# Gathering and scaling the first expert's 32 slots ahead of the other 96, with the number of rounds read behind that

## The chip, the cores and the metric

The kernel runs on one core of one Trainium2 chip. The metric is the device time of one execution in microseconds (us); lower is better.

## What is computed

Two layers of a decoder trunk on 256 tokens of width 1024, all in float32. Each layer is a mixer of three attentions and then a mixture of experts (64 experts of width 256, two experts for each token), each followed by a LayerNorm:

```python
def reference(x, ...):
    for l in range(DEPTH):                       # DEPTH = 2
        mix = hybrid_mixer(x, w_in[l], ..., w_out[l])
        x = layer_norm(ALPHA * x + mix, ln1_g[l], ln1_b[l])
        ffn = moe_ffn(x, router_w, router_b, moe_w1[l], moe_w3[l], moe_w2[l])
        x = layer_norm(ALPHA * x + ffn, ln2_g[l], ln2_b[l])
    return x

def moe_ffn(x, router_w, router_b, w1, w3, w2):
    e_idx, gates = route(x, router_w, router_b)  # top-1 group of 8 experts, top-2 experts in it
    # for each expert e, over the tokens that chose it:
    #   h = silu(xb @ w1[e]) * (xb @ w3[e]);  y += gate * (h @ w2[e])
```

The change touches only the start of the expert stage.

## The kernel before

**Batches.** The 64 experts are worked through in batches of NB = 4, with BLK = 32 token slots for each expert, so P = 128 slots a batch: slots 0 to 31 are the first expert's, 32 to 63 the second's, and so on. 16 batches hold all experts; if an expert has more than 32 tokens, all batches are gone through again (a round). The number of batches is therefore known only once the tokens are counted. VectorE works it out (lines 1679 to 1682) and writes it into `iters`; every engine then reads it into a register with `start_batches` (lines 361 to 366), which waits for `routed` and loads the register (a TENSOR_LOAD in the trace). The loops over batches run up to that register.

**What a batch does on TensorE.** It gathers the batch's tokens: for each of DC = 8 chunks of 128 features, a matmul with the stream x as the weights and the one-hot matrix `chosen` (tokens by slots) as the moving operand, over NT = 2 tiles of 128 tokens. VectorE and ScalarE scale the result by the first LayerNorm's columns into `xg`. Then, for each expert, gate and up matmuls (32 slots as weights, w1 and w3 moving, four column groups of the array side by side), a fold over these groups, silu, a turn of the hidden rows, the down matmuls with w2, and `add_all` (line 1197), which adds the rows to the output in PSUM. The gather of the next batch is done inside each batch. Each float32 matmul is two instructions in the trace.

**The first batch** is written out by hand (`first_batch`, line 1202). Its gather is `gather_first` (line 1024): token tile 0 early, while the router still works on tile 1, and tile 1 when the choice is known. Its chunks lie in four PSUM banks (`first_bank`). Chunks 0, 1, 4 and 5 are scaled by VectorE and 2, 3, 6 and 7 by ScalarE, all 128 slots at once (`scale_first`). `first_up_gate` (line 1106) multiplies the first expert's 32 slots, first with w1 (gate, line 1119) and then with w3 (up, line 1124), in bank 2. `up_gate` (line 1092) does experts 1 to 3 (line 1102).

**Weights.** SyncE issues all weight transfers in one hand-written order. Two sets of buffers (even and odd batches) hold the weights of a batch, 12.6 MB. Batches 0 and 1 are loaded during the attention stage. The refills wait on TensorE:

```python
                def load_first(j, back, e, parity, last=False, by_matrix=False):
                    for k in range(NB):
                        if by_matrix and k == 0:
                            after(sp, l, gate_first, 1)
                            load_w13(e, k, parity, matrices=(0,))
                        done = 2 * (k // 2) + 2 if last else k + 1
                        sp.wait_ge(part_psum.sem, (b0 + j) * NB + (part_psum.start + done - back))
```

So the first matrix of batch 2 is loaded as soon as the first expert's gate matmuls are done (`gate_first`), its second when its up matmuls are done (`part_psum`), the next expert's when that expert's are done, w2 after the down matmuls. Batch 3's w1 and w3 (line 509) wait for batch 1's second expert.

## Time and profile before

| | |
|---|---|
| median of 3 runs | 1150.59 us (1150.25 to 1151.67) |
| profiled execution, its own time | 1149.66 us |
| its span | 1147.9 us |
| TensorE busy (matmul) | 1046.3 us, 91% of the span |
| TensorE busy (weight load) | 534.3 us, 47% |
| VectorE, ScalarE busy | 403.6 us, 260.3 us |
| DMA | 441.05 MB, 384 GB/s in the mean |

The span is that of the instructions; the execution's own time is 1.8 us longer. The page cuts the span into 40 slices of 28.7 us: slices 6 to 19 and 27 to 39 are the two expert stages. PE stands for TensorE, PEld for its weight loads, DVE for VectorE, ACT for ScalarE, SP for SyncE; an SPq row is an issue of DMAs by SyncE. Matmuls overlap, so the spacing of a row of them is its length over their count and not the duration of one.

### The profile page before, as it was taken

Reading aid. Unit: us, or ns where it says so; the run is one execution under the profiler, and the core shown is the slowest. Engines: PE = TensorE matmul, PEld = TensorE weight load, DVE = VectorE, ACT = ScalarE, POOL = GpSimd, SP = SyncE. Lnnn points to the kernel's source line nnn. Section 1 sums busy time; section 2 is a strip of 40 time slices with the busy share of each in tenths; the row PEclk is TensorE's granted clock in tenths of the full one; section 3 lists DMA queues with packets and bytes.
Section 4 is the critical chain, followed back from the end, with each engine's and each line's share of the span. In section 5 each row is a group of like instructions: output and inputs, shape, how many; then the busy total and the mean of one; then the engine's idle time right before and its main releaser. Section 6 shows DMA issues by size and latency. Waiting matters only on the chain.

```text
span 1147.9 us, 26691 instructions
## 1 busy us (share of the span) xinstructions
PE 1046.3 (91%) x11382; PEld 534.3 (47%) x11382; DVE 403.6 (35%) x1189; ACT 260.3 (23%) x683; POOL 18.7 (2%) x36
## 2 busy tenths in 40 slices
PE   9999999989889988888899999989889989988888
PEld 5665753434444443333466657434344444433333
DVE  4865532222222221222268656322222222222213
ACT  1245321111121111111131544121221111111111
POOL 0010000000000000000000100000000000000000
PEclk9999999999999999999999999999999999999999
DMA  9967699999999999999996677999999999999997
GB/s 307 330 249 293 256 400 406 428 426 425 426 428 429 429 429 429 429 429 420 387 319 227 268 297 278 403 426 425 426 426 429 428 428 429 428 429 428 429 421 268
DMA packets 72861, 441.05 MB, mean 384 GB/s; under 512 B 16480, under 2 KB 36064, under 8 KB 43616
## 3 DMA queue, kind: packets, MB, share of 16 engines
q1 hardware_dynamic: 72512, 439.52, 93.6%
q8 instruction: 46, 0.75, 0.3%
q0 software_dynamic: 144, 0.58, 0.1%
q14 instruction: 15, 0.12, 0.0%
q10 hardware_dynamic: 144, 0.07, 0.0%
HBM read 439.10 MB, written 1.05 MB: 383 GB/s over the span
## 4 chain that ended last, share of the span: by engine, by line
PE 73%; SPq 9%; DMA 9%; DVE 6%; issue 2%; ACT 1%; POOL 0%; DVEq 0%
PE bank L1087 13%; PE bank L1172 12%; PE bank L1184 8%; PE bank L693 8%; DMA w_odd<-in_moe_w 8%; PE bank L1069 7%; SPq L401 5%; PE bank L819 4%; PE bank L1102 3%; SPq L540 3%; PE bank L1137 2%; PE bank L1178 2%; DVE moe L1745 1%; PE bank L1056 1%; PE bank L963 1%
## 5 line engine op out<-in xcount | busy, mean ns | idle before, releaser
L1808 ACT ACTIVATE moe<-bank 128x512 f32<-128x512 f32 (+2 forms) x164 | 84.2, 523 | 555.8 <-PE bank L1087 275.5
L1709 DVE COPY moe<-bank 128x512 f32<-128x512 f32 x64 | 44.3, 692 | 315.6 <-PE bank L1087 256.9
L1184 PE MATMUL bank<-moe 128*128 128x512 f32 (+1 forms) x264 | 119.3, 593 | 23.6 <-DVE moe L1745 22.5
L1172 PE MATMUL bank<-w_even,moe 64*32 64x512 f32 x896 | 99.0, 590 | 10.1 <-DVE moe L1729 10.1
L1087 PE MATMUL bank<-w_odd,moe 64*32 64x512 f32 x1536 | 92.8, 629 | 11.2 <-issue 6.1
L1069 PE MATMUL bank<-moe,x 128*64 128x64 f32 x3072 | 98.3, 224 | 2.6 <-issue 2.6
L1069 PEld LDWEIGHTS bank<-moe,x 128*64 128x64 f32 x3072 | 94.8, 138 | 6.8 <-issue 6.8
L1745 DVE COPY moe<-bank 128x512 f32<-128x512 f32 x32 | 22.1, 692 | 198.7 <-PE bank L1172 178.0
L1184 PEld LDWEIGHTS bank<-moe 128*128 128x128 f32 x264 | 47.3, 190 | 96.0 <-DVE moe L1745 48.9
L1172 PE MATMUL bank<-w_odd,moe 64*32 64x512 f32 x768 | 84.8, 590 | 7.5 <-DVE moe L1729 7.5
L1087 PE MATMUL bank<-w_even,moe 64*32 64x512 f32 x1536 | 86.1, 591 | 5.9 <-issue 5.9
L693 PE MATMUL bank<-w_even,w_odd 128*128 128x384 f32 x240 | 81.3, 489 | 0.0
L1965 ACT ACTIVATE moe<-bank,small 128x64 f32<-128x64 f32 x192 | 59.3, 414 | 90.3 <-PE bank L1069 90.3
L1087 PEld LDWEIGHTS bank<-w_odd,moe 64*32 64x32 f32 x1536 | 30.2, 112 | 71.7 <-issue 71.7
L1172 PEld LDWEIGHTS bank<-w_even,moe 64*32 64x32 f32 x896 | 32.8, 107 | 65.5 <-issue 65.5
L1646 DVE TENSOR_SCALAR moe<-bank,small 128x64 f32<-128x64 f32 x192 | 50.6, 337 | 22.8 <-PE bank L1069 22.8
L693 PEld LDWEIGHTS bank<-w_even,w_odd 128*128 128x128 f32 x240 | 44.6, 190 | 29.1 <-issue 2.0
L1137 PE MATMUL bank<-moe,constants 128*32 128x512 f32 (+1 forms) x272 | 34.5, 576 | 25.3 <-DVE moe L1709 20.9
L1087 PEld LDWEIGHTS bank<-w_even,moe 64*32 64x32 f32 x1536 | 28.5, 107 | 61.7 <-issue 61.7
L1172 PEld LDWEIGHTS bank<-w_odd,moe 64*32 64x32 f32 x768 | 28.1, 107 | 54.9 <-issue 54.9
L1808 ACT ACTIVATE w_odd<-bank 128x256 f32<-128x256 f32 (+3 forms) x60 | 27.8, 468 | 83.2 <-PE bank L651 27.4
L819 PE MATMUL bank<-w_odd 128*128 128x512 f32 x96 | 44.8, 602 | 0.0
(203 smaller groups left out, 1013.5 us busy)
## 6 DMA issues: line engine op xcount, KB each, us to landing
w_even<-in_moe_w SPq DMA_DIRECT2D x76, 2048.0 KB, 36.4
w_odd<-in_moe_w SPq DMA_DIRECT2D x72, 2048.0 KB, 34.3
w_odd<-in_moe_w SPq DMA_DIRECT2D x44, 1024.0 KB, 10.2
w_even<-in_moe_w SPq DMA_DIRECT2D x40, 1024.0 KB, 9.6
w_even<-in_w_in SPq DMA_DIRECT2D x24, 768.0 KB, 11.0
w_odd<-in_w_out SPq DMA_DIRECT2D x4, 2048.0 KB, 13.6
w_odd<-in_moe_w SPq DMA_DIRECT2D x8, 512.0 KB, 11.1
w_even<-in_w_in SPq DMA_DIRECT2D x4, 416.0 KB, 6.8
```

What stands on the lines that cost most here:

```text
L401: sp.dma_start(w13_slots[parity][k][:, m, :, :].rearrange("p c f -> p (c f)"), (w1, w3)[m][l * NE + e * NB + k]).then_inc(sig.sem, 16)
L693: last = mm(to[:, 0:GW], rows[:, c, :], weights[:, c, :], start=fresh and c == 0, stop=c == DC // 2 - 1, skip_group_check=True)
L819: last = mm(mix_bank[t][h][:, :], oT[:, c, t * P:(t + 1) * P], w_out_half[h][:, c, :], start=c == 0, stop=c == DC - 1, skip_group_check=True)
L1069: last = mm(bank[2 + h][64 * z:64 * z + 64, 64 * c:64 * c + 64], xc_pair[:, t, h, c, :], chosen_pair[:, t, z], start=t == 0, stop=t == 1)
L1087: last = mm(bank[2 * q + z][BLK * i:BLK * (i + 1), :], xg_pair[rows, c, BLK * q:BLK * (q + 1)], w[rows, :, c, :], start=c < 4, stop=c >= 2 ...
L1137: last = mm(to[BLK * k:BLK * (k + 1), 0:cols.stop - cols.start], const("fold"), partial[:, k, cols], start=True, stop=True)
L1172: last = mm(bank[h][BLK * k:BLK * (k + 1), :], hT_pair[rows, c, BLK * q:BLK * (q + 1)], w2_pairs[parity][q][rows, c, 512 * h:512 * h + 512 ...
L1184: return mm(Y[t][h][:, lo - 512 * h:hi - 512 * h], scatter[:, t * P:(t + 1) * P], y_rows[:, lo:hi], start=False, stop=True, skip_group_che ...
L1646: last = ts(xg_pair[:, c, :], bank[2][:, 64 * c:64 * c + 64], pair_cols[:, 0, c:c + 1], pair_cols[:, 1, c:c + 1], ALU.mult, ALU.add)
L1709: nc.vector.tensor_copy(partial[:, k, :], source[:, :]).then_inc(part_dve.sem, 1)
L1808: return fn(dst, src, ACT.Copy)
L1965: last = fn(xg_pair[:, DC + c, :], bank[3][:, 64 * c:64 * c + 64], ACT.Identity, scale=pair_cols[:, 0, DC + c:DC + c + 1], bias=pair_cols[ ...
```

## The change

The first batch's gather of token tile 1 is split by slots. The first expert's 32 slots of all 8 chunks are gathered first, scaled (VectorE chunks 0 to 3, 6 and 7, ScalarE 4 and 5) and multiplied with the gate matrix. Between the gate and the up matmuls stands the gather of the other 96 slots. VectorE works out the number of rounds behind the first scales; a signal `counted` tells TensorE that bank 0 has been read. The remaining scales (VectorE chunks 0 to 3, ScalarE 4 to 7) must be done before the second expert. The register with the number of batches is read by SyncE behind the issues for batches 2 and 3, by TensorE behind the first batch, and by VectorE and ScalarE behind their scales. Chunks 2 and 3 move from bank 3 to the other half of bank 2, and the first expert's products from bank 2 to bank 3.

```diff
--- before.py
+++ after.py
@@ -265,7 +265,7 @@
         turn_bank = [bank[i] for i in (4, 5, 4, 5, 7, 7, 7, 7)]
         score_bank, pT_bank, o_bank = [bank[i] for i in (2, 3, 6, 7)], bank[4:6], bank[6]
         mix_bank = [bank[0:2], bank[2:4]]
-        first_bank = [bank[2], bank[3], bank[1][:, 2 * P:], bank[0][:, 2 * P:]]
+        first_bank = [bank[2], bank[2][:, 2 * P:], bank[1][:, 2 * P:], bank[0][:, 2 * P:]]
         Y = [[bank[4 + 2 * t + n] for n in range(2)] for t in range(NT)]
 
         class Signal:
@@ -321,8 +321,9 @@
         chosen_ok, xg_dve, xg_act = Signal("chosen_ok"), Signal("xg_dve"), Signal("xg_act")
 
         gate_first = Signal("first_gate_matrix_used", 1)
-        first_mid, first_late = Signal("first_batch_mid", 1), Signal("first_batch_late", 1)
-        first_begin_sb, first_mid_sb = Signal("first_batch_begin_sb", 1), Signal("first_batch_mid_sb", 1)
+        counted, first_late = Signal("tokens_counted", 1), Signal("first_batch_late", 1)
+        first_slots, first_slots_dve, first_slots_act = (
+            Signal("first_slots_psum", 3), Signal("first_slots_dve", 3), Signal("first_slots_act", 1))
         gathered = Signal("gathered_first_half"), Signal("gathered_second_half")
         part_psum, part_dve, part_act = Signal("part_psum", start=2 * NB), Signal("part_dve"), Signal("part_act")
         gu_psum, eg_ok, hn_ok = Signal("gu_psum"), Signal("eg_ok"), Signal("hn_ok")
@@ -489,7 +490,7 @@
                 load_w2(1, 1, 1)
                 after(sp, l, z_psum, 2)
                 load_w2(1, 0, 1)
-                m, b0 = start_batches(sp, base, l)
+                b0 = batches_before(sp, base)
 
                 def load_first(j, back, e, parity, last=False, by_matrix=False):
                     for k in range(NB):
@@ -525,6 +526,7 @@
                 load_w2_pairs(2, 0)
                 load_batch(3, 2 * NB, 3, 1)
                 load_w2_pairs(3, 1)
+                m, b0 = start_batches(sp, base, l)
                 with sp.Fori(4, m, 2) as j_even:
                     for parity in range(2):
                         j = j_even + parity
@@ -1021,19 +1023,22 @@
                 route(1, (4, 5), 7)
                 route(1, (6, 7), 8)
 
-                def gather_first(t):
+                def gather_first(t, lo, hi):
                     for c in range(DC):
-                        if c == 6:
-                            after(pe, l, *((routed, 1) if t else (z_lin, 2)))
-                        last = mm(first_bank[c // 2][:, c % 2 * P:(c % 2 + 1) * P], xc[:, t, c, :], chosen[:, t, :],
-                                  start=t == 0 and c in (0, 2), stop=t == 1, skip_group_check=True)
-                        if t == 1 and c % 2:
-                            last.then_inc((gathered[0], first_mid, first_late, gathered[1])[c // 2].sem, 1)
+                        if c == 6 and lo == 0:
+                            after(pe, l, *((counted, 1) if t else (z_lin, 2)))
+                        last = mm(first_bank[c // 2][:, c % 2 * P + lo:c % 2 * P + hi], xc[:, t, c, :],
+                                  chosen[:, t, lo:hi], start=t == 0 and c == 0, stop=t == 1, skip_group_check=True)
+                        if t == 1 and c in (3, 5, 7):
+                            if lo == 0:
+                                last.then_inc(first_slots.sem, 1)
+                            else:
+                                last.then_inc((gathered[0], first_late, gathered[1])[c // 2 - 1].sem, 1)
 
 
                 after(pe, l, n_ready, 1)
                 after(pe, l, chosen_first, 1)
-                gather_first(0)
+                gather_first(0, 0, P)
                 turn_rows(0)
                 keep_warm(7, bank[7])
                 after(pe, l, picked, 2)
@@ -1046,7 +1051,7 @@
                 keep_warm(2, bank[7])
                 after(pe, l, n_ready, 2)
                 pe.wait_ge(chosen_ok.sem, batches_before(pe, base) + 1)
-                gather_first(1)
+                gather_first(1, 0, BLK)
 
                 def gather(b):
 
@@ -1107,21 +1112,18 @@
                     pe.wait_ge(w13_in[0][0].sem, b0 * 8 + (32 + 32 * l))
                     w = w13_slots[0][0]
                     for c in range(DC):
-                        if c == 0:
-                            after(pe, l, first_begin_sb, 1)
-                        elif c == 2:
-                            after(pe, l, first_mid_sb, 1)
-                        elif c == 4:
-                            pe.wait_ge(xg_dve.sem, b0 + 1)
-                        elif c == 6:
-                            pe.wait_ge(xg_act.sem, b0 + 1)
+                        if c == 4:
+                            after(pe, l, first_slots_act, 1)
+                        elif c % 2 == 0:
+                            after(pe, l, first_slots_dve, c // 2 + 1 if c < 4 else 3)
                         q = c % 4
-                        last = mm(bank[2][BLK * q:BLK * (q + 1), 0:FE], xg[:, c, 0:BLK], w[:, 0, c, :],
+                        last = mm(bank[3][BLK * q:BLK * (q + 1), 0:FE], xg[:, c, 0:BLK], w[:, 0, c, :],
                                   start=c < 4, stop=c >= 4, skip_group_check=True)
                     last.then_inc(gate_first.sem, 1)
+                    gather_first(1, BLK, P)
                     for c in range(DC):
                         q = c % 4
-                        last = mm(bank[2][BLK * q:BLK * (q + 1), FE:2 * FE], xg[:, c, 0:BLK], w[:, 1, c, :],
+                        last = mm(bank[3][BLK * q:BLK * (q + 1), FE:2 * FE], xg[:, c, 0:BLK], w[:, 1, c, :],
                                   start=False, stop=c >= 4, skip_group_check=True)
                     last.then_inc(part_psum.sem, 1)
 
@@ -1201,6 +1203,8 @@
 
                 def first_batch():
                     first_up_gate()
+                    pe.wait_ge(xg_dve.sem, b0 + 1)
+                    pe.wait_ge(xg_act.sem, b0 + 1)
                     up_gate(0, 0, 1, 32 + 32 * l)
                     after(pe, l, seed_act, 1)
                     seed_rows(0)
@@ -1291,8 +1295,9 @@
                         after(pe, l, third_summed, t + 1)
                         add_rows(t, *fourth).then_inc(y_added.sem, 1)
 
+                b0 = batches_before(pe, base)
+                first_batch()
                 m, b0 = start_batches(pe, base, l)
-                first_batch()
                 batch(0, 1, 32 + 32 * l, pairs=False, next_pairs=False)
                 batch(2, 0, 48 + 32 * l)
                 batch(2, 1)
@@ -1676,22 +1681,25 @@
                 v.wait_ge(chosen_ok.sem, b0 + 1)
 
                 after(v, l, rank_psum, 3)
-                link(nc.vector.tensor_reduce(red[:, 0:1], bank[0][:, 2 * NE:3 * NE], X, ALU.max))
+                signal(nc.vector.tensor_reduce(red[:, 0:1], bank[0][:, 2 * NE:3 * NE], X, ALU.max), counted, 1)
+                after(v, l, cols_in, 160)
+
+                def scale_first(c, lo, hi):
+                    return ts(xg[:, c, lo:hi], first_bank[c // 2][:, c % 2 * P + lo:c % 2 * P + hi], g_cols[:, 0, c:c + 1],
+                              g_cols[:, 1, c:c + 1], ALU.mult, ALU.add)
+
+                for i, c in enumerate((0, 2, 6)):
+                    after(v, l, first_slots, 3 if c == 6 else 1)
+                    scale_first(c, 0, BLK)
+                    scale_first(c + 1, 0, BLK).then_inc(first_slots_dve.sem, 1)
                 link(ts(v1[:, 0, 0:MAX_ROUNDS - 1], const("thresholds"), red[:, 0:1], None, ALU.is_lt))
                 link(nc.vector.tensor_reduce(red[:, 1:2], v1[:, 0, 0:MAX_ROUNDS - 1], X, ALU.add))
                 signal(ts(iters[:, :], red[:, 1:2], float(BATCHES), float(BATCHES - 2), ALU.mult, ALU.add), routed, 1)
                 weigh_scores(1)
-                after(v, l, cols_in, 160)
-                def scale_first(c):
-                    return ts(xg[:, c, :], first_bank[c // 2][:, c % 2 * P:(c % 2 + 1) * P], g_cols[:, 0, c:c + 1],
-                              g_cols[:, 1, c:c + 1], ALU.mult, ALU.add)
-
                 v.wait_ge(gathered[0].sem, b0 + 1)
-                scale_first(0)
-                scale_first(1).then_inc(first_begin_sb.sem, 1)
-                after(v, l, first_late, 1)
-                scale_first(4)
-                scale_first(5).then_inc(xg_dve.sem, 1)
+                for c in range(4):
+                    last = scale_first(c, BLK, P)
+                last.then_inc(xg_dve.sem, 1)
                 m, b0 = start_batches(v, base, l)
 
                 def batch(j, last_of_all, e_next, first=False, pairs=False, w13_pairs=False, next_pairs=False):
@@ -1705,7 +1713,7 @@
                         choose_next()
                     for k in (0, 2):
                         v.wait_ge(part_psum.sem, b * NB + (part_psum.start + k + 1))
-                        source = bank[k if w13_pairs else 2 if first and k == 0 else 0]
+                        source = bank[k if w13_pairs else 3 if first and k == 0 else 0]
                         nc.vector.tensor_copy(partial[:, k, :], source[:, :]).then_inc(part_dve.sem, 1)
                         if first and k == 0:
                             weights(1)
@@ -1956,7 +1964,7 @@
                 route(1)
                 after(act, l, cols_in, 160)
                 seeds(0, range(DC))
-                m, b0 = start_batches(act, base, l)
+                b0 = batches_before(act, base)
 
                 def copy_gathered(g, pairs=False):
                     act.wait_ge(gathered[1].sem, g + 1)
@@ -1971,16 +1979,20 @@
                                   scale=g_cols[:, 0, c:c + 1], bias=g_cols[:, 1, c:c + 1])
                     last.then_inc(xg_act.sem, 1)
 
-                def scale_first(c):
-                    return fn(xg[:, c, :], first_bank[c // 2][:, c % 2 * P:(c % 2 + 1) * P], ACT.Identity,
+                def scale_first(c, lo, hi):
+                    return fn(xg[:, c, lo:hi], first_bank[c // 2][:, c % 2 * P + lo:c % 2 * P + hi], ACT.Identity,
                               scale=g_cols[:, 0, c:c + 1], bias=g_cols[:, 1, c:c + 1])
 
-                after(act, l, first_mid, 1)
-                scale_first(2)
-                scale_first(3).then_inc(first_mid_sb.sem, 1)
+                after(act, l, first_slots, 2)
+                scale_first(4, 0, BLK)
+                scale_first(5, 0, BLK).then_inc(first_slots_act.sem, 1)
+                after(act, l, first_late, 1)
+                scale_first(4, BLK, P)
+                scale_first(5, BLK, P)
                 act.wait_ge(gathered[1].sem, b0 + 1)
-                scale_first(6)
-                scale_first(7).then_inc(xg_act.sem, 1)
+                scale_first(6, BLK, P)
+                scale_first(7, BLK, P).then_inc(xg_act.sem, 1)
+                m, b0 = start_batches(act, base, l)
 
                 def copy_partial(b, k, source=bank[1]):
                     act.wait_ge(part_psum.sem, b * NB + (part_psum.start + k + 1))
```

## Rows read from the trace of the kernel before

**Rows 1.** The page: the span, and GB/s of the DMA in 40 slices.

```profile
span 1147.9 us, 26691 instructions
...
GB/s 307 330 249 293 256 400 406 428 426 425 426 428 429 429 429 429 429 429 420 387 319 227 268 297 278 403 426 425 426 426 429 428 428 429 428 429 428 429 421 268
```

**Rows 2.** The chain that ended last: start us, us, what.

```profile
125.97 1.73 PE bank L974 x16
...
149.56 1.72 PE bank L1102 x14
...
172.47 3.44 PE bank L1184 x8
175.90 7.05 PE bank L1102 x64
...
545.28 19.30 DMA w_odd<-in_moe_w
...
713.28 1.79 PE bank L1028 x16
715.07 1.49 PE bank L1119 x14
...
1112.89 19.04 DMA w_odd<-in_moe_w
```

**Rows 3.** Timeline of SyncE's issues: start us, us, what.

```profile
148.74 8.97 SPq L401 DMA_DIRECT2D w_even<-in_moe_w  x8
...
179.61 4.23 SPq L509 DMA_DIRECT2D w_odd<-in_moe_w  x4
193.24 0.80 SPq L411 DMA_DIRECT2D w_odd<-in_moe_w  x2
201.57 4.15 SPq L509 DMA_DIRECT2D w_even<-in_moe_w  x4
...
716.82 8.97 SPq L401 DMA_DIRECT2D w_even<-in_moe_w  x8
...
746.15 4.23 SPq L509 DMA_DIRECT2D w_odd<-in_moe_w  x4
```

**Rows 4.** Windows: engines' busy us, last three columns granted clock, DMA share, GB/s.

```profile
148.50:150.50 2.00, 2.00 (x30) 0.88 (x24) 0.85 (x3) 0.00 (x0) 0.00 (x0) 1.00 0.46 86
179.60:182.00 2.40, 2.40 (x28) 0.78 (x24) 0.69 (x1) 0.54 (x1) 0.00 (x0) 1.00 0.67 164
746.00:748.50 2.50, 2.50 (x31) 0.74 (x24) 0.69 (x1) 0.60 (x1) 0.00 (x0) 1.00 1.03 439
151.28:179.61 28.33, 26.39 (x224) 13.66 (x228) 7.70 (x23) 5.48 (x14) 0.00 (x0) 0.94 1.02 429
719.36:746.15 26.79, 24.85 (x224) 13.46 (x228) 7.70 (x23) 5.48 (x14) 0.00 (x0) 1.00 1.00 417
```

**Rows 5.** Timeline of the first batch's start, layer 0; in brackets idle before, releaser.

```profile
144.86 1.95 PE L1028 MATMUL bank<-moe,x 128*128 128x128 f32 x16
...
145.87 1.37 DVE L1686 TENSOR_SCALAR moe<-bank,small 128x128 f32<-128x128 f32 x4
146.52 1.50 ACT L1975 ACTIVATE moe<-bank,small 128x128 f32<-128x128 f32 x4 [1.43 <-PE bank L1028]
...
148.07 0.11 PEld L1119 LDWEIGHTS bank<-w_even,moe 128*32 128x32 f32 x2 [0.45 <-ACT moe L1975]
...
148.98 0.60 PE L1102 MATMUL bank<-w_even,moe 128*32 128x512 f32 x2
```

**Rows 6.** Timeline: the first batch's down matmuls, layer 0 and layer 1.

```profile
161.59 5.17 PE L1178 MATMUL bank<-w_even,moe 128*32 128x512 f32 x32 [0.81 <-DVE moe L1729]
...
729.67 3.64 PE L1178 MATMUL bank<-w_even,moe 128*32 128x512 f32 x32 [0.81 <-DVE moe L1729]
```

**Rows 7.** Timeline: scales of a later batch, 64 columns each.

```profile
209.02 2.11 DVE L1646 TENSOR_SCALAR moe<-bank,small 128x64 f32<-128x64 f32 x8 [0.97 <-PE bank L1069]
```

**Rows 8.** Tile iters, up to 160 us: engine op, ns min/median/max, starts.

```profile
L365 PEldq TENSOR_LOAD <-iters x1: 500/500/500, 145.8 to 145.8; - x1
```

## Prediction

> **What bounds the kernel now.** I read the page first [rows 1]: the DMA engines move 425 to 429 GB/s through nearly all of both expert stages, while TensorE is seldom idle either (the table above). Two resources are that close to full, so the question is which one ends each stage. The chain [rows 2] shows it at the end of a layer: TensorE waits for pieces of the last w2, which land at 545.28 + 19.30 = 564.58 us in layer 0 and at 1112.89 + 19.04 = 1131.93 us in layer 1. The chain walks back from there through the DMA queue. So the weight stream ends the layer, and a layer can only finish earlier if that stream starts earlier or pauses less.
>
> Next I read when SyncE issues [rows 3]. The refill of the first batch's buffers (batch 2's weights) starts at 148.74 and 716.82 us; the refill behind batch 1 (batch 3's weights) at 179.61 and 746.15 us. The DMA windows [rows 4] tell which of them finds the stream empty: 86 GB/s in 148.5:150.5 and 164 GB/s in 179.6:182 are pauses, 439 GB/s in 746:748.5 is not. From the second refill to the last landing it is 564.58 - 179.61 = 384.97 us in layer 0 and 1131.93 - 746.15 = 385.78 us in layer 1. The two are equal but for 0.8 us, which I read as follows: layer 0's stream had run dry and restarts with the issue; layer 1's still had about 0.8 us of transfers in hand. So the end of a layer hangs on the later of two things: when the stream runs on from its first refill, and when batch 1 on TensorE frees the second set of buffers. In layer 0 the second decides already; in layer 1 it is 0.8 us from deciding. Everything between the first gather and 179.61 is TensorE's chain, without slack: gate, up, fold, hidden layer, down, gather, add, batch 1 [rows 2, 6].
>
> **The change part by part.** All times are of layer 0; layer 1 runs the same 568 us later [rows 2, 3].
>
> *The first gather.* Before, 16 instructions of 128 columns run from 144.86 to 146.81 us [rows 5]. After, they move 32 columns. The nearest rows are those with the same 128x128 weights and 64 moving columns: L974, 16 in 1.73 us in the chain [rows 2], 108 ns each, hardly less than the 112 ns with 128 columns (L1028, 1.79 us for 16). Halving the columns saved almost nothing, so I take 108 ns for 32 too, 1.73 us; the other bound is proportional to columns, 28 ns, 0.45 us. It then ends near 146.7 and saves about 0.1 us. The Trainium skill, "TensorE: Matmul & The Clock Gate", section "LDWEIGHTS (loading the stationary operand)", says that loading weights costs by weight columns, columns / 1.2 in ns, which is 107 ns for 128; the trace's 108 ns agrees. The same page's "Back-to-back issue gap" gives a lone matmul's gap by its moving columns instead; by that the sum would be another one, and it is a rival below.
>
> *The scales.* Before, VectorE works out the rounds first (L1679 to L1682, then L1605) and scales from 145.87; ScalarE waits for the rounds and its register load until 146.52, and TensorE's last wait for ScalarE ends at 148.07 [rows 5]. After, VectorE has the count at 144.92 and waits only for chunk 3, about 145.9. Its spacing is (1.37 - 0.40) / 3 = 0.32 us at 128 columns and (2.11 - 0.34) / 7 = 0.25 at 64 [rows 5, 7], so some 0.22 at 32 with 0.30 for the last: six operations end at 145.9 + 5 x 0.22 + 0.30 = 147.3, and with the wait for chunk 7 at 147.45. ScalarE's two (0.35 spacing at 128) end at about 147.1. The last pair of gate matmuls starts at 147.45 in place of 148.07: **0.6 us earlier**, and the first refill is issued at 148.1. Bounds: 0.2 (scales cost as at 128) to 0.8 us.
>
> *The second gather.* 16 more instructions between gate and up matmuls: 1.73 us by the same row, 1.3 by moving columns alone (96 of 128), 1.9 with a change of weight shape at either side. The up matmuls end at 149.56, where L1102 goes on alone [rows 2], - 0.6 + 1.75 = 150.7, **1.2 us later**. Behind them TensorE now waits for all slots of all chunks. ScalarE scales 4 and 5 from about 149.2, then 6 and 7: 3 x 0.33 + 0.44 = 1.4, so 150.6. Before, expert 1's matmuls were already let in at 148.98 while the up matmuls still ran [rows 5]; this overlap goes. I add 0.1 and take **+1.3 us** for TensorE from expert 1 on; bounds 0.9 and 1.7.
>
> *The register loads.* A load takes 0.50 us [rows 8], and from the rounds, done just ahead of L1605 and so near 145.57, to ScalarE's first work [rows 5] it is 0.95. TensorE's moves behind the first batch: it lies under add_all, whose 8 matmuls keep the array busy for 3.44 us with no gap to the next batch (L1184 ends where L1102 begins). In the trace it starts at 145.8, while the gather's matmuls run, and in layer 1 the gather ends at 715.07 and the gate begins at 715.07 [rows 2]. I take 0; if it isn't covered, up to 1.2 us a layer. SyncE's moves behind two w2 issues at 193.24, and the next issue is at 201.57 [rows 3]: 7.5 us of cover. ScalarE's and VectorE's run until 151.6 and 151.0; ScalarE's next input comes when expert 1 is done (151.28 before [rows 2], 152.6 after), VectorE's copy of expert 0 starts 0.2 us late, and its reader is expert 2, behind expert 1 and the seeding of the output. Nothing.
>
> *The stream.* The first refill's first megabyte flows 0.6 us earlier and takes 1.05 MB / 428 GB/s = 2.45 us, from about 149.9 to 152.35. The next needs the up matmuls (150.7) and flows after the 1.8 us seen from issue to flow (148.74 to 150.5): 152.5. The gap is 0.2 us, and the stream stands 0.4 us ahead. That is the whole gain, and it counts only where the first refill decides.
>
> *The sum.* Layer 0: the second refill decides, +1.3 us. Layer 1: +1.3 less the 0.8 us in hand, +0.5 us. Together **+1.8 us** on the profiled execution's own 1149.66 us (span 1147.9): 1151.5. The median of the runs shown is 0.9 us above that execution, so the forecast is 1150.59 + 1.8 = **1152.4 us**. A difference within 0.2%, 2.3 us, is about what can't be told from none.
>
> **The rivals.**
>
> *Slower: the clock falls in a first batch once more.* In layer 0 the granted clock is 0.94 over 151.28:179.61, in layer 1 it is 1.00, with the same work: 28.33 against 26.79 us [rows 4]. The down matmuls took 5.17 us against 3.64 [rows 6]; the clock fell to 1.2 GHz after TensorE had waited for the hidden layer. These waits move by 1.3 us against the earlier part. If layer 1's first batch is hit too, +1.5 and the 0.8 no longer covers: 1.8 + 1.5 = 3.3, 1153.9 us. It decides over 0.2% by itself, as soon as 0.5 us of it stays. For it: it happened in one of two layers. Against: only one.
>
> *Slower: TensorE's register load isn't hidden.* +0.95 to 1.2 us in both layers on top: 1154.1. Against it stands the gapless start of layer 1's gate.
>
> *Faster: the clock is spared in layer 0.* +1.3 - 1.5 = -0.2 there, +0.5 in layer 1: 1150.9.
>
> *Faster: the earlier first refill decides.* If my reading of the 385 us is wrong and the stream has several us in hand at the second refill, TensorE's delay is swallowed and the 0.6 us counts twice: 1149.4. For it: DMA is full almost everywhere. Against it: 164 GB/s in 179.6:182.
>
> *Gathers cost by moving columns* (the skill's isolated gap). The first gather ends near 145.4, the scales by 146.7, the gate 1.3 us earlier; the second costs 1.3: TensorE +0.1 us, the stream 1.2 us ahead. Layer 0 about 0, layer 1 -0.7: 1149.9. The L974 row speaks against it.
>
> *It doesn't do what it says*: scales of 32 columns cost like those of 128, the gate gains 0.2 us, TensorE is +1.7: +1.7 + 0.9 = 2.6, 1153.2.
>
> **How the numbers follow.** Forecast 0.46 (own range 1151.4 to 1153.4, its upper tail over 0.2%); clock once more 0.15; register load 0.05; no shorter scales 0.08; clock spared 0.11; early refill 0.09; moving columns 0.06. From these: slower by over 0.2% 0.34 (0.28 of the cases and 0.06 of the forecast's tail), faster by over 0.2% 0.07 (two of the faster cases together), the rest 0.59. The range that leaves out no more than 2 in 10 is 1149.8 to 1154.3.
>
> **What would show it.** L1028's group should have 32-column instructions at some 108 ns spacing, and 96-column ones at the same. SyncE's first refill at about 0.6 us earlier after the gather's start; expert 1's matmuls 1.3 us later; the second refill 1.3 us later, with a longer DMA pause in layer 0 and a new one in layer 1; from it to the last landing still 385.0 us. I am wrong if the second refill is later and the last landing isn't, or if a new gap stands ahead of batch 1's first matmul.

## The result: 5.9 us slower

| | before | changed |
|---|---|---|
| median of 18 runs | 1150.90 us (1147.95 to 1156.92) | 1156.94 us (1152.72 to 1162.48) |
| ratio | | 1.0051, 95% interval 1.0037 to 1.0065 |

The kernel became 0.51% slower (0.0051 x 1150.9 = 5.9 us). The forecast was +1.8 us (1152.4) with a range up to 1154.3: the time lies outside it and is more than three times the forecast step. The profiled execution took 1157.68 us (span 1155.9) at a mean granted clock of 0.990, and the 18 runs spread over 9.8 us, so one profile against one profile (+8.0 us of span) can't be added up to the median; the rows below are read place by place.

The first batch of layer 0 in the changed kernel's timeline (start us, length, engine, line, operation, in brackets the idle time before and what ended it; `...` marks rows left out). Its gather starts at 145.35, 0.49 us later than before [rows 5]; take that off to compare. L1030 is the gather, L1120 gate, L1126 up, L1107 the second expert, L1688 and L1983 the scales:

```profile
145.35 1.87 PE L1030 MATMUL bank<-moe,x 128*128 128x32 f32 x16
146.47 1.41 DVE L1688 TENSOR_SCALAR moe<-bank,small 128x32 f32<-128x32 f32 x6 [1.05 <-PE bank L1030]
146.82 0.64 ACT L1983 ACTIVATE moe<-bank,small 128x32 f32<-128x32 f32 x2 [1.25 <-PE bank L1030]
...
147.93 0.14 PEld L1120 LDWEIGHTS bank<-w_even,moe 128*32 128x32 f32 x4 [0.20 <-DVE moe L1688]
...
148.49 1.86 PEld L1030 LDWEIGHTS bank<-moe,x 128*128 128x128 f32 x16 [0.41 <-issue]
148.49 2.02 PE L1030 MATMUL bank<-moe,x 128*128 128x96 f32 x16
149.73 1.23 DVE L1688 TENSOR_SCALAR moe<-bank,small 128x96 f32<-128x96 f32 x4 [1.07 <-PE bank L1030]
150.10 1.40 ACT L1983 ACTIVATE moe<-bank,small 128x96 f32<-128x96 f32 x4 [2.64 <-PE bank L1030]
150.44 0.59 PEld L1126 LDWEIGHTS bank<-w_even,moe 128*32 128x32 f32 x16
...
151.57 0.19 PEld L1107 LDWEIGHTS bank<-w_even,moe 128*32 128x32 f32 x8 [0.54 <-DVE moe L1688]
...
151.60 1.92 PE L1107 MATMUL bank<-w_even,moe 128*32 128x512 f32 x16
...
153.45 0.77 PE L990 MATMUL bank<-constants,moe 64*128 64x64 f32 x10
```

The gather of 32 columns takes 1.87 us, much as that of 128 took (1.95 [rows 5]). The last gate pair starts at 147.93 - 0.49 = 147.44. The second gather costs another 1.95 us up to 150.44. Expert 1 can't start before ScalarE's last scale, 150.10 + 1.40 = 151.50; the row names VectorE, but its scales had ended at 150.96, so it was ScalarE. Expert 1's 16 instructions end at 151.60 + 1.92 - 0.49 = 153.03 against 151.28 [rows 2], 1.75 us later.

SyncE's issues, both layers (start, length):

```profile
148.60 11.37 SPq L402 DMA_DIRECT2D w_even<-in_moe_w  x8
169.29 0.81 SPq L412 DMA_DIRECT2D w_even<-in_moe_w  x2
182.01 4.23 SPq L510 DMA_DIRECT2D w_odd<-in_moe_w  x4
...
720.50 11.36 SPq L402 DMA_DIRECT2D w_even<-in_moe_w  x8
739.51 1.26 SPq L412 DMA_DIRECT2D w_even<-in_moe_w  x2
752.23 4.23 SPq L510 DMA_DIRECT2D w_odd<-in_moe_w  x4
```

From the first to the second refill it is now 33.41 and 31.73 us, before 30.87 and 29.33 [rows 3]: +2.5 and +2.4. The gather of layer 1 starts at 717.26 in place of 713.12, so 4.14 us have to be taken off there. After its gather the first refill is then 0.6 and 0.5 us earlier, and the second 1.9 us late in both layers.

Windows of the stream in the kernel before, from 1 us ahead of the first refill (columns as in [rows 4], the last one GB/s):

```profile
147.74:190.74 43.00, 39.73 (x352) 20.34 (x348) 13.07 (x39) 9.12 (x22) 0.00 (x0) 0.96 0.97 396
190.74:390.74 200.00, 180.95 (x2594) 81.17 (x2588) 48.94 (x139) 37.32 (x96) 0.00 (x0) 1.00 1.01 427
390.74:549.74 159.00, 136.83 (x1887) 63.77 (x1884) 36.94 (x106) 27.26 (x71) 0.00 (x0) 0.98 1.01 427
715.82:758.82 43.00, 39.73 (x368) 20.66 (x364) 13.07 (x39) 9.12 (x22) 0.00 (x0) 1.00 0.97 402
```

The same windows of the changed kernel:

```profile
147.60:190.60 43.00, 40.16 (x353) 21.48 (x351) 14.20 (x45) 8.73 (x21) 0.00 (x0) 0.96 0.94 377
190.60:390.60 200.00, 181.06 (x2593) 81.47 (x2596) 49.89 (x143) 38.27 (x98) 0.00 (x0) 1.00 1.01 428
390.60:549.60 159.00, 136.56 (x1892) 62.34 (x1892) 36.38 (x106) 27.22 (x72) 0.00 (x0) 0.97 1.01 427
719.50:762.50 43.00, 39.63 (x362) 21.77 (x364) 15.24 (x49) 9.85 (x25) 0.00 (x0) 1.00 0.96 387
```

After the first 43 us the stream holds 427 GB/s in both kernels. Within them it loses 43 x (1 - 396/427) = 3.1 and 2.5 us before, 5.0 and 4.0 us after: 3.4 us more in the two layers. It starts 0.6 and 0.5 us earlier, so the stream as a whole is 2.3 us later. That is near the forecast's 1.8. The larger part of the loss has to be somewhere else.

The ends of the layers show where. The issues of the piece of the last w2 whose landing the prediction read, in the changed kernel, each with the profile's line on its DMA (the last figure is the us from issue to landing):

```profile
547.39 8.97 SPq L542 DMA_DIRECT2D w_odd<-in_moe_w  x1
w_odd<-in_moe_w SPq DMA_DIRECT2D x1, 512.0 KB, 19.3
...
1118.02 8.97 SPq L542 DMA_DIRECT2D w_odd<-in_moe_w  x1
w_odd<-in_moe_w SPq DMA_DIRECT2D x1, 512.0 KB, 19.1
```

TensorE's last rows of each layer's expert stage, two of the kernel before and two of the changed one:

```profile
570.57 1.13 PE L1184 MATMUL bank<-moe 128*128 128x256 f32 x4 [0.50 <-ACT moe L1808]
1137.80 1.13 PE L1184 MATMUL bank<-moe 128*128 128x256 f32 x4 [0.50 <-ACT moe L1808]
...
574.09 1.13 PE L1186 MATMUL bank<-moe 128*128 128x256 f32 x4 [0.50 <-ACT moe L1816]
1146.01 1.13 PE L1186 MATMUL bank<-moe 128*128 128x256 f32 x4 [0.50 <-ACT moe L1816]
```

The piece lands at 566.7 and 1137.1, less 0.49 and 4.14: 1.6 and 1.1 us late. TensorE ends at 574.09 - 0.49 against 570.57 and at 1146.01 - 4.14 against 1137.80: 3.0 and 4.1 us late. So in these two executions TensorE ends both layers later than the stream's lateness explains, by 1.4 and 3.0 us.

### The profile page after: what moved, and what is told of

Same layout as the page of the kernel before. It is cut to its first block, busy times and chain, and to the rows that moved or that the text cites. A ratio compares the mean times of both kernels' runs of the same rounds, so it can differ in the third digit from the quotient of the medians.

```text
span 1155.9 us, 26782 instructions
## 1 busy us (share of the span) xinstructions
PE 1052.2 (91%) x11414; PEld 539.5 (47%) x11414; DVE 405.9 (35%) x1201; ACT 261.3 (23%) x687; POOL 18.7 (2%) x36
## 4 chain that ended last, share of the span: by engine, by line
PE 84%; DVE 7%; DMA 5%; issue 3%; ACT 1%; SPq 0%; another core or an unknown queue 0%; POOL 0%; DVEq 0%; ACTq 0%
PE bank L1092 15%; PE bank L1174 15%; PE bank L1186 10%; PE bank L695 8%; PE bank L1074 8%; PE bank L1107 4%; DMA w_odd<-in_moe_w 4%; PE bank L821 4%; PE bank L1139 3%; PE bank L1180 2%; PE bank L684 2%; PE bank L1061 2%; DVE moe L1753 2%; DVE moe L1717 1%; PE bank L965 1%
## 5 line engine op out<-in xcount | busy, mean ns | idle before, releaser
L1174 PE MATMUL bank<-w_even,moe 64*32 64x512 f32 x896 | 99.2, 590 | 10.1 <-DVE moe L1737 10.1
L1092 PE MATMUL bank<-w_even,moe 64*32 64x512 f32 x1536 | 92.4, 624 | 10.9 <-issue 10.9
L1092 PE MATMUL bank<-w_odd,moe 64*32 64x512 f32 x1536 | 89.0, 607 | 10.7 <-issue 6.1
L1174 PE MATMUL bank<-w_odd,moe 64*32 64x512 f32 x768 | 84.8, 590 | 7.5 <-DVE moe L1737 7.5
```

The costliest lines, as they stand in the source:

```text
L1092: last = mm(bank[2 * q + z][BLK * i:BLK * (i + 1), :], xg_pair[rows, c, BLK * q:BLK * (q + 1)], w[rows, :, c, :], start=c < 4, stop=c >= 2 ...
L1174: last = mm(bank[h][BLK * k:BLK * (k + 1), :], hT_pair[rows, c, BLK * q:BLK * (q + 1)], w2_pairs[parity][q][rows, c, 512 * h:512 * h + 512 ...
```

## The experiments

Every kernel was timed against the kernel before on the same chip. A is the theory of the prediction (the stream sets a layer's end), B that TensorE's own lateness costs, C that the rounds and register reads cost, D that the stream's lateness costs more than its length. E and F came later.

**e1_delay8 and e2_delay16: only a delay.** The kernel before, and in `first_up_gate`:

```diff
                     last.then_inc(gate_first.sem, 1)
+                    keep_warm(8, bank[7])      # 16 in e2_delay16
```

> The kernel before, with 8 idle matmuls (16 instructions of 128 columns, as long as the second gather) between the first expert's gate and up matmuls in both layers, and nothing else. Theory A (TensorE's delay before the second refill reaches the end once per layer, less what layer 1's stream has in hand): expert 1 about 1.9 us later, time +2.7 to +3.8 us. Theory B (the delay costs more than itself, because TensorE then also finishes each layer later behind the stream, with clock falls): +5 to +7 us, with TensorE work after the last landing longer than before. Theory C (the loss of the change comes from its other part, rounds and register reads): below +2.5 us.

> The same with 16 idle matmuls, expert 1 about 3.7 us later. Theory A: +6 to +7.4 us, in proportion to the delay. Theory B: +9 to +13 us. Theory C: as A.

Measured: e1 1157.73 us, ratio 1.0072 (1.0056 to 1.0088; all intervals here are 95%); e2 1160.47 us, 1.0096 (1.0078 to 1.0113), against 1150.68 us. The first delay costs about 7 us, the second one 2.7 more. A delay of the second gather's length alone makes the whole loss, so C isn't needed for it. A's ranges are too low for both. B's hold e2, and e1 lies at their upper edge; but the second step of 2.7 us is nearer A's 3.3 than B's 4 or more. With 6 and 4 runs that step is uncertain by some 2 us, so it decides little.

**e3_rounds_only: only the moved rounds and register reads.** The diff's lines for `counted`, `start_batches` and the three operations of the rounds, with the gather and its scales whole (`weigh_scores(1)` stands ahead of the scales).

> Only the second part of the change: the gather stays whole with all scales of 128 columns as before, but the rounds are worked out behind the scales and all engines read the register as late as in the change. Theories A and B: ScalarE no longer waits for the register, the gate ends 0.3 to 0.6 us earlier, nothing is added: 0 to -1.5 us, the second refill 0.3 to 0.6 us earlier. Theory C: slower by 2 us or more, with a gap on TensorE ahead of batch 1 or a later issue of batch 4's weights.

Measured: 1150.61 us, 1.0000 (0.9984 to 1.0015). In layer 0 ScalarE starts its scales 1.09 us after the gather's start in place of 1.66, but takes 1.70 us for them in place of 1.50 [rows 5], and the first refill is 0.37 us earlier after the gather's start. It costs nothing (C falls), and the earlier refill brings nothing that can be measured.

**e4_up_then_gather.** The changed kernel with the second gather behind the up matmuls:

```diff
                     last.then_inc(gate_first.sem, 1)
-                    gather_first(1, BLK, P)
...
                     last.then_inc(part_psum.sem, 1)
+                    gather_first(1, BLK, P)
```

> The changed kernel with the second gather behind the up matmuls in place of ahead of them. Expert 1 waits for the same scales, now about 1.1 us later behind the gather, so TensorE's delay at the second refill grows from 1.9 to about 2.9 us, while the second matrix of batch 2 is loaded 2 us earlier. Theory A: 1 to 2 us slower than the changed kernel. Theory B: 2 to 3 us slower than it. If the pause of the stream between its first two matrices is what costs, it is faster than the changed kernel.

Measured: 1157.10 us, 1.0066 (1.0048 to 1.0084). It can't be told from the changed kernel, where A and B both expected it slower by 1 to 3 us. It isn't faster either, but that says little of the pause between the refill's first two matrices: in the first 43 us its stream moves 368 and 380 GB/s against the changed kernel's 377 and 387, so the pause has only moved.

**e5_stream_late: only the second refill late.** In `load_pairs`, for batch 3's first pair alone:

```diff
-  sp.wait_ge(part_psum.sem, ... + (part_psum.start + 2 * q + 2 - back))
+  sp.wait_ge(part_psum.sem, ... + (part_psum.start + 2 * q + 3 - back))   # q == 0 only
```

> The kernel before, with SyncE's second refill (batch 3's first pair) held until batch 1's third expert is done in place of its second, 1.7 us later in both layers; TensorE's work and order are untouched. Theory A (the stream sets the end of a layer, and a late second refill reaches the end in full, less what is in hand): +2.5 to +3.5 us. Theory B (TensorE's own lateness matters): 0 to +1 us. Theory D (the stream's lateness is what costs, but more than its length, as the last batches' waits and clock falls come to lie worse): +5 us or more.

Measured: 1153.69 us against 1150.63, 1.0026 (1.0014 to 1.0037), +3.1 us, the size that A gave. The profile, of its slowest run (1157.20), shows more than A's mechanism: the clock is at half in 530:533 and 1100:1103, and TensorE's last down matmuls wait for no weight in either layer. So the 3.1 us needn't be the stream's alone.

**e6_tensor_late: only TensorE late, behind the second refill.** The kernel before, with:

```diff
+                keep_warm(8, bank[0])
                 batch(2, 0, 48 + 32 * l)
```

> The kernel before, with 8 idle matmuls (16 instructions, about 1.8 us) on TensorE behind batch 1, after the second refill has been issued, in both layers. Theory A: 0, within 1 us either way, since TensorE has a lead over the stream later on. Theory B: +3 to +7 us, like the same matmuls in the first batch. Theory D: 0.

Measured: 1152.54 us, 1.0019 (1.0006 to 1.0032), +1.9 us. A expected nothing within 1 us, B at least 3: both missed. TensorE's lateness costs something by itself (by the interval 0.7 to 3.7 us), beside the stream's. That 3.1 and 1.9 add up to something near 5.9 proves nothing, since e5's 3.1 may hold both.

**e7_before_early and e8_after_early: the second refill earlier.** The first matrix half of a pair fills the buffer of one expert of batch 1, so it can be issued when that one is done. Once on the kernel before, once on the changed one:

```diff
                         for m_ in range(2):
+                            if early:       # batch 3 alone
+                                sp.wait_ge(part_psum.sem, ... + (part_psum.start + 2 * q + m_ + 1 - back))
```

> The kernel before, with batch 3's pair loads split by matrix: the first half of each pair is issued when one expert of batch 1 is done, 1.7 us before the second half. Theory A: the second refill is 1.7 us earlier, layer 0's pause of the stream goes; -0.5 to -2.5 us. Theory B: 0. Theory D: -1 to -4 us.

> The changed kernel with the same split of batch 3's pair loads. Theory A: the 1.9 us by which its second refill is late are taken back: -3 to -3.5 us against the changed kernel, so +2 to +3 us over the kernel before if 5.9 is right for the change, or less. Theory B: no gain, still +5 to +6 us over the kernel before. Theory D: within 1 us of the kernel before.

Measured: e7 1149.65 us, 0.9996 (0.9983 to 1.0009), which can't be told from the kernel before; e8 1153.23 us, 1.0025 (1.0013 to 1.0036). The changed kernel gets 1156.94 - 1153.23 = 3.7 us back (3.4 when each is set against the kernel before timed beside it), as A says. What is left is +2.6 us. It is of e6's size; that it is TensorE's lateness isn't shown by this run.

**e9 to e12: idle matmuls in every paired batch.** Theory E: TensorE waits some 3.1 us for weights late in a layer; where the clock falls after the last such wait, TensorE ends the layer behind the stream. To keep it busy in part of the wait:

```diff
                 def up_gate_pair(j, parity, q):
+                    if q == 1:
+                        keep_warm(8, bank[2])
```

e9 is the kernel before with it, e10 the changed one, e11 is e7 with it, and e12 is e11 with e3's moved rounds.

> The kernel before, with 8 idle matmuls (1.75 us) in each paired batch between the two expert pairs, where TensorE waits 3.1 us for the stream late in a layer. TensorE has 3.3 us a batch to spare against the stream, and the idle wait shrinks to 1.35 us, so the clock shouldn't fall there. Theory E (the late clock falls after 3.1 us waits put TensorE behind the stream's end in some executions): mean clock 0.996 or more, time -0.5 to -2 us against the kernel before, spread of the runs halved. If those falls are harmless: no change in time, +0 to +1 us.

> The changed kernel with the same 8 idle matmuls. Theory E: the falls that follow the change's different alignment go, and what is left of the loss against e9 is the stream's part alone, +2.5 to +3.5 us. If the rest of the loss (about 3 us) comes from something else than falls late in the layer, it stays: +5 to +6 us against e9.

> The kernel before with batch 3's pair loads split by matrix (as e7) and the 8 idle matmuls (as e9), a candidate for a faster kernel. Theory E and A: -1 us from the earlier second refill on top of e9, so 2 to 3 us faster than the kernel before. Else as e7, -1 us.

> e11 with the rounds and register reads moved behind the scales (as e3), the gather left whole. TensorE's first batch and the first refill are 0.4 to 0.6 us earlier: with the second refill early too, the stream as a whole starts that much earlier in both layers, -0.8 to -1.2 us against e11. If the first refill's time doesn't reach the end: equal to e11.

Measured against 1149.78 us: e9 1175.10, e10 1179.49, e11 1175.04 and e12 1178.39 us, all 2.2 to 2.6% slower. I had misjudged TensorE's spare time: 3.3 us a batch is true only once it has caught up with the stream. The idle matmuls are 12 x 1.75 = 21 us a layer, and in the kernel before its waits of over 0.9 us late in layer 0 are only 3.08, 1.46, 3.03 and 1.44 us. These kernels have become slower by TensorE's added work and say nothing of E. They do show that TensorE isn't far from being the bound.

**e13 to e15: the idle matmuls only in a layer's last paired batch.** The same lines, for `batch(m, 0)` alone, on the kernel before (e13), the changed one (e14) and e6 (e15). Theory F: the falls are harmless.

> The kernel before, with 8 idle matmuls (1.75 us) only in the last paired batch of a layer, ahead of its second pair. Theory E (the clock fall after the last 3.1 us wait leaves TensorE behind the stream's end): the wait there is 1.4 us or less, no fall follows it, 0 to -1.5 us against the kernel before. Theory F (falls there are harmless): 0 to +1 us.

> The changed kernel with the same 8 idle matmuls in the last paired batch. Theory E: against e13 only the stream's part is left, +2.5 to +3.5 us. Theory F: still +5 to +6 us against e13.

> e6 (8 idle matmuls behind batch 1, TensorE 1.8 us late behind the second refill) with the 8 idle matmuls in the last paired batch. Theory E: within 0.7 us of e13. Theory F: +1.5 to +2.5 us against e13, as e6 against the kernel before.

Measured against 1151.61 us: e13 1152.14 us, 1.0008 (0.9993 to 1.0022); e14 1153.55 us, 1.0024 (1.0009 to 1.0039); e15 1152.09 us, 1.0006 (0.9992 to 1.0020). TensorE's lateness, worth 1.9 us in e6, shows no cost here (e15 against e13, -0.1 us), though with 12 runs each a cost up to about 1.4 us isn't excluded. The change costs 1.9 us by the medians (e14; 1.4 against e13) in place of 5.9. That is E's word on e15; e14's is below what E gave. E's word on e13 is missed: the kernel before gains nothing from the idle matmuls.

The traces show what differs. TensorE's timeline of the kernel before around the last wait of layer 0:

```profile
528.09 2.38 PE L1087 MATMUL bank<-w_even,moe 64*32 64x512 f32 x40 [1.44 <-issue]
```

and the windows there and in layer 1, with the granted clock last but two:

```profile
530.00:533.00 3.00, 2.14 (x42) 0.56 (x24) 0.69 (x1) 0.60 (x1) 0.00 (x0) 1.00 0.97 415
1095.00:1098.00 3.00, 2.70 (x56) 1.27 (x64) 0.00 (x0) 0.00 (x0) 0.00 (x0) 1.00 0.97 410
```

TensorE's timeline of the changed kernel (the last two rows are its last down matmuls):

```profile
530.18 1.11 PE L1092 MATMUL bank<-w_even,moe 64*32 64x512 f32 x8 [3.31 <-issue]
...
566.09 2.36 PE L1180 MATMUL bank<-w_odd,moe 128*32 128x512 f32 x24 [0.52 <-DVE moe L1737]
...
570.75 1.07 PE L1180 MATMUL bank<-w_odd,moe 128*32 128x256 f32 x16
```

and its windows behind the waits of both layers:

```profile
530.00:533.00 3.00, 2.81 (x32) 1.02 (x40) 0.00 (x0) 0.00 (x0) 0.00 (x0) 0.50 0.99 421
1100.50:1103.50 3.00, 2.91 (x32) 1.01 (x40) 0.00 (x0) 0.00 (x0) 0.00 (x0) 0.50 1.00 426
```

TensorE's timeline of e6, whose wait is longer still:

```profile
527.67 2.81 PE L1087 MATMUL bank<-w_even,moe 64*32 64x512 f32 x24 [4.44 <-DMA w_even<-in_moe_w]
```

and its windows:

```profile
527.00:530.00 3.00, 2.33 (x24) 0.76 (x32) 0.00 (x0) 0.00 (x0) 0.00 (x0) 0.50 0.99 421
530.00:533.00 3.00, 3.00 (x48) 0.88 (x32) 0.00 (x0) 0.00 (x0) 0.00 (x0) 0.65 0.95 401
```

With the short wait the clock stayed at 2.4 GHz; after 3.31 and 4.44 us of waiting it was 1.2 GHz (0.50), and the batch's next matmuls ran at half speed (in e6 a window later the mean is 0.65, so the clock came back within it). In layer 1 the changed kernel's wait was 3.08 us, the kernel before's 1.48. The changed kernel then does its last down matmuls with no wait for a weight: it is behind the stream. The length of a wait doesn't decide alone: after 3.03 us ahead of 498.72 the kernel before fell to half clock, after 3.03 us ahead of 500.65 the changed one didn't, and e7 didn't after 3.15 us ahead of 525.70. e15's list of waits for the same place (who waits, us, times, longest) has one for the stream:

```profile
PE bank L1180 <- DMA w_odd<-in_moe_w: 1.3, 1, 1.3
```

**e16_early_lastwarm, e17_after_early_lastwarm, e18_rounds_early_lastwarm: both remedies.** The idle matmuls of the last paired batch on e7 (e16), on e8 (e17) and on e7 with the moved rounds (e18).

> e7 (batch 3's pair loads split by matrix) with the 8 idle matmuls in the last paired batch, a candidate for a faster kernel. Theory E: -1 us against e13, so 1 to 2.5 us faster than the kernel before. Theory F: as e7, -1 us against the kernel before.

> The changed kernel with batch 3's pair loads split by matrix and the 8 idle matmuls in the last paired batch. Stream's part as reckoned (the second refill's delay is all of it): within 1 us of e16, as the first refill's 0.6 us a layer is a gain then. If the later refills inside the first batch (second matrix, w2) also leave pauses in the stream: 1 to 3 us slower than e16.

> e16 with the rounds and the register reads moved behind the scales and the gather left whole (as e3). The first batch and the first refill are 0.4 to 0.6 us earlier in both layers: -0.8 to -1.2 us against e16, 2 to 3 us faster than the kernel before. If the moved rounds are worth nothing, as e3 showed without the remedies: equal to e16.

Measured: e16 1150.17 us against 1151.61, 0.9991 (0.9978 to 1.0003); e17 1153.67 us against 1150.64, 1.0019 (1.0006 to 1.0032); e18 1151.03 us, 0.9998 (0.9986 to 1.0011). e16 has the lowest median against its kernel before, but its interval includes 1, so no version here is shown to beat the kernel before. With the idle matmuls, the earlier refill takes nothing more off the changed kernel (e17 against e14), though it takes 2.0 us off the kernel before (e16 against e13), and the moved rounds are worth nothing (e18). e17 stays 3.5 us behind e16, beyond the 1 us of its first branch. The second branch blamed later pauses in the stream, but the first 43 us don't show them: 402 and 402 GB/s in e17, 407 and 401 in e16.

## Why the prediction was wrong, point by point

- **The first gather: right.** 1.87 us for 16 instructions of 32 columns (forecast 1.73); with these 128x128 weights 32, 96 and 128 columns took 1.87, 2.02 and 1.95 us. The weight loads' own rows carry it: 1.86 us for 16 beside 96 columns, 1.87 before. The rival by which gathers cost by moving columns is out. The Trainium skill, "TensorE: Matmul & The Clock Gate", section "LDWEIGHTS (loading the stationary operand)", has weight loads cost by weight columns; the trace agrees in kind, at 117 ns each.
- **The gate 0.6 us earlier: right** (147.44 against 148.07, the first refill 148.60 - 0.49 = 148.11 against 148.74; in layer 1 the refill is 0.5 us earlier).
- **TensorE +1.3 us from expert 1 on: too small.** It is 1.75, just above the bounds. The second gather took 1.95 us where I had 1.73, its first weight load comes 0.56 us after the last gate pair's, and ScalarE's last scale ends at 151.01 after correction where I had 150.6. At the second refill it is 1.9 in both layers.
- **The register loads cost nothing: right** (e3).
- **The stream's part: right in mechanism, a little small.** Forecast 1.8, read from the windows 2.3 and from the landings 1.6 + 1.1 = 2.7. The sign "still 385.0 us" came true: 566.7 - 182.01 = 384.7 and 1137.1 - 752.23 = 384.9. The piece read there is the third of six; in the changed kernel the last lands 4.5 us behind it.
- **That layer 1 has 0.8 us in hand was an accident of one execution.** The half clock in the first batch makes that difference: first to second refill takes 30.87 and 29.33 us in the profile of before, but 29.34 and 29.34 in e6's and 29.34 and 31.04 in e13's, whose first batches are the same. In this pair it held: in layer 1 the second refill is 1.9 us late and the piece of w2 1.1.
- **The step that failed** is the one in "What bounds the kernel now": that the end of a layer hangs on the stream alone ("the later of two things", both of which act through the stream). I took TensorE as idle in reserve behind the second refill, so that its own lateness could only count through the refills. The runs showed that stream and TensorE end a layer nearly together: in the kernel before, TensorE waits only some 0.3 us for weights in its last down matmuls of either layer (in layer 0, 24 of them take 2.70 us in place of 2.36). In the changed kernel it doesn't wait there at all and ends the layers 3.0 and 4.1 us later, with the stream 1.6 and 1.1 late. TensorE late by itself costs 1.9 us (e6), and the change's 5.9 us shrink to 1.9 once the last long wait is broken up (e14). The clock rival I had, 0.15 for one more fall, looked at the first batch only; the falls at the end of these layers come after the last wait.
- Two numbers of the rivals don't follow from their rows. No faster rival lies over 0.2% below 1150.59 (the lowest is 1149.4), so the 0.07 for faster by over 0.2% had no case behind it. The register load's 0.95 to 1.2 us in both layers gives 1154.3 to 1154.8 us and not 1154.1.
- The refill-to-landing time of 385 us could have warned me only of the stream. What would have warned me was to ask how long TensorE waited for the pieces of the last w2: the chain of [rows 2] goes to the DMA there by some 0.3 us.

What stays open. That the falls are the cause of the larger part rests on e14, on e6 against e15, and on the profiles above; a kernel that removes the falls and nothing else wasn't made, since the idle matmuls also take time in the last paired batch (perhaps why e13 isn't faster). Against it stands e4: its profile (1156.70 us) has the clock at full speed behind the last wait of both layers (531:534 and 1101:1104), and it is as slow as the changed kernel. Why the first delay of 1.9 us (e1) costs 7 us and the second 2.7 isn't settled. Their profiles, one each, fit the falls: behind the last wait e1's clock is at half in both layers (530:533 and 1100:1103), e2's at full in both (532:535 and 1104:1107). That the length and place of the waits decide whether a fall comes last is argued, not shown. Nor is it settled why e17 isn't faster than e14, and what its 3.5 us over e16 are.

## What to carry to other kernels

When two resources are both near full, read at the end of a stage how long the one that seems to spare waits for the other: if it is tenths of a us, a delay of either counts. This gather with 128x128 float32 weights didn't get cheaper by fewer moving columns, so splitting it by columns doubled it. A delay of the first batch moved the second refill here, and with it the end of the stream. And a difference between two like layers in one profile can be one execution's clock: look at a second profile before reckoning with it.

## What the runs showed of the hardware

- 128x128 float32 weights: 16 instructions take 1.87 us with 32 moving columns, 2.02 with 96, 1.95 with 128.
- The same kernel varied by 9 us from run to run on one core (1147.95 to 1156.92), and in the changed kernel the time goes with the mean granted clock: 1152.72 us at 0.996, 1162.48 at 0.987. Late in a layer the falls shown stood behind waits of TensorE of some 3 us and more, and not behind each of these: 3.03 us ahead of 500.65 in the changed kernel had none, 3.31 ahead of 530.18 had one. Layer 0's first batch had one (0.50 in 161.3:164.7 of the kernel before) with waits of only 1.13 and 0.81 us.
- One layer's expert stage moved weights at 427 GB/s for 359 us on end; the stream's lost time lay in the first 43 us after the refills began.
